# Two directions of a gated linear attention: the second one's gates, scan and keys are issued among the first one's states, in buffers of their own

## The reference, cut to what matters

```python
def gla_chunked(q, k, v, log_a, s0):
    ...
    b = jnp.cumsum(la, axis=3)
    b_last = b[:, :, :, -1:, :]
    q_in = qc * jnp.exp(b)
    k_in = kc * jnp.exp(-b)
    k_end = kc * jnp.exp(b_last - b)
    a_intra = jnp.where(lower, jnp.einsum('bhncd,bhnsd->bhncs', q_in, k_in), 0.0)
    o_intra = jnp.einsum('bhncs,bhnse->bhnce', a_intra, vc)
    chunk_state = jnp.einsum('bhnsd,bhnse->bhnde', k_end, vc)
    chunk_decay = jnp.exp(b_last[:, :, :, 0, :])
    s_final, s_enter = lax.scan(step, s0, (...))
    o_inter = jnp.einsum('bhncd,nbhde->bhnce', q_in, s_enter)
...
    la_cf = gla_log_decay(zac_f, wa2_f, ba_f)      # log_sigmoid(z @ w2 + b2) / 16
    o_f, _ = gla_chunked(Q, K, V, gla_log_decay(za_f, wa2_f, ba_f), s_f)
    o_b, _ = gla_chunked(flip(Q), flip(K), flip(V), flip(gla_log_decay(za_b, wa2_b, ba_b)), s_b)
    y = gla_output(o_f + flip(o_b), g, norm_g)
```

## Time and profile before

| | |
|---|---|
| median of 3 runs | 4089.5 us (4086.95 to 4093.19) |
| profiled execution | 4082.31 us, span 4080.5 us |
| PE busy | 3818.6 us (94%) |
| DVE, ACT, POOL busy | 2399.2, 1682.2, 739.6 us |

### The profile page before, as it was taken

The page is one execution under the profiler, slowest core; times in us unless marked ns, Lnnn a source line. Parts: engine busy times, 40 slices in busy tenths (PEclk is TensorE's granted clock), DMA queues, the critical chain, the costliest instruction groups (busy, mean ns, idle before and its releaser), DMA issues. The chain is left out here.

```text
span 4080.5 us, 57384 instructions
## 1 busy us (share of the span) xinstructions
PE 3818.6 (94%) x23037; PEld 3308.2 (81%) x23037; DVE 2399.2 (59%) x4212; ACT 1682.2 (41%) x2809; POOL 739.6 (18%) x582
## 2 busy tenths in 40 slices
PE   8999989989888879999999999997999999799998
PEld 5788767777787879999999999775777877677887
DVE  6455323447879767777777777556643345674333
ACT  4523332444456883333333333436532233554222
POOL 0112000253104513222233222201000010101000
PEclk9999999989999999999999999998999999899999
DMA  5211334433345459888888887321143432202332
GB/s 206 69 40 43 112 132 176 166 97 92 111 144 166 163 187 307 292 278 285 284 275 287 278 289 226 119 69 52 54 134 114 144 124 89 63 30 83 97 94 78
DMA packets 209193, 617.30 MB, mean 151 GB/s; under 512 B 18464, under 2 KB 68640, under 8 KB 205088
## 3 DMA queue, kind: packets, MB, share of 16 engines
q1 hardware_dynamic: 168352, 465.76, 35.2%
q0 software_dynamic: 40576, 147.87, 10.4%
HBM read 583.67 MB, written 29.88 MB: 150 GB/s over the span
## 5 line engine op out<-in xcount | busy, mean ns | idle before, releaser
L510 DVE TENSOR_TENSOR wlo<-raw,whi 128x1024 fp32r<-128x1024 f32 x576 | 714.7, 1241 | 704.8 <-ACT whi L502 704.2
L544 PE MATMUL ps<-hhi,whi 128*128 128x512 f32 (+1 forms) x2824 | 1075.2, 381 | 12.3 <-ACT uact L3372 8.9
L546 PE MATMUL ps<-hlo,whi 128*128 128x512 f32 (+1 forms) x2824 | 1049.2, 372 | 0.4 <-DVE hlo L2609 0.4
L502 ACT ACTIVATE whi<-raw 128x1024 fp32r<-128x1024 f32 x660 | 693.4, 1054 | 605.4 <-PE ps L555 455.6
L555 PE MATMUL ps<-hhi,wlo 128*128 128x512 f32 (+1 forms) x2824 | 663.2, 373 | 0.0
L544 PEld LDWEIGHTS ps<-hhi,whi 128*128 128x128 f32 x2824 | 533.1, 189 | 115.3 <-issue 22.7
L546 PEld LDWEIGHTS ps<-hlo,whi 128*128 128x128 f32 x2824 | 533.4, 189 | 68.9 <-issue 3.6
L555 PEld LDWEIGHTS ps<-hhi,wlo 128*128 128x128 f32 x2824 | 511.5, 188 | 72.1 <-issue 4.8
L544 PE MATMUL ps<-ag_hi,whi 128*128 128x384 f32 x1024 | 342.1, 334 | 0.0
L546 PE MATMUL ps<-ag_lo,whi 128*128 128x384 f32 x1024 | 342.0, 334 | 0.0
L510 POOL TENSOR_TENSOR wlo<-raw,whi 128x1024 fp32r<-128x1024 f32 x85 | 209.2, 2468 | 328.9 <-ACT whi L502 328.0
(11 more groups left out here) (629 smaller groups left out, 6160.2 us busy)
## 6 DMA issues: line engine op xcount, KB each, us to landing
raw<-w_in SPq DMA_DIRECT2D x151, 512.0 KB, 3.7
raw<-peer_u SPq DMA_DIRECT2D x128, 512.0 KB, 4.6
raw<-peer_v SPq DMA_DIRECT2D x128, 512.0 KB, 4.3
raw<-w_mod SPq DMA_DIRECT2D x96, 512.0 KB, 3.7
raw<-w_gate SPq DMA_DIRECT2D x66, 512.0 KB, 3.6
raw<-w_up SPq DMA_DIRECT2D x66, 512.0 KB, 3.5
raw<-w_down SPq DMA_DIRECT2D x66, 512.0 KB, 3.5
gate_dram<-stage SPq DMA_DIRECT2D x24, 1024.0 KB, 4.7
```

The costliest lines, as they stand in the source:

```text
L502: a.x.activation(whi[n % NW][:], raw[i % NRAW][:], ACT.Copy, bias=0.0, scale=1.0).then_inc(*a.gives("hi", i))
L510: e.x.tensor_tensor(wlo[n % NW][:], raw[i % NRAW][:], whi[n % NW][:].bitcast(F32), ALU.subtract).then_inc(*e.gives(*lo_sig(i)))
L544: t.x.matmul(o, w, p.hi, start=grp.opens and k == 0, stop=False)
L546: t.x.matmul(o, w, p.lo, start=False, stop=False)
```

## The change

The parts of the stream become named steps, and one function, used by all engines, sets their order. Gates and scan of direction 1 (`gates(1)`, `decays(1)`) are laid down around the chunk states of direction 0, its keys (`ends(1)`, `turning(1)`) before direction 0's mix. kin and qin of direction 1 (`keys(1)`) stay behind direction 0's mix, which reads the same two tiles; their multiplication moves into `sums(1)`. Direction 1 has C in the tile gvT (the untransposed values, free once they are turned) and a `dec` of its own. The mark "qk done", which lets `values` 0 begin, moves behind `sums(1)`. No instruction is added or removed in the kernel's code but loads of ACT's function table, which follow from the order: 81 in the program against 79.

```diff
-            self.dec = sb(f"{name}_dec", 8.5 if lat else 8.75, [2, self.NCH])
+            self.dec, self.dec2 = [sb(f"{name}_dec{i}", kb, [2, self.NCH]) for i, kb in
+                                   enumerate((8.5, 8.6875) if lat else (8.75, 8.8125))]
...
+        decs, Cs = [m.dec, m.dec2], [m.C, m.gvT]
+
+        def order(values_by_token, gates, decays, ends, turning, sums, entered, mix, keys):
+
+            yield from values_by_token()
+            yield from gates(0)
+            yield from decays(0)
+            yield from keys(0)
+            yield from ends(0)
+            yield from turning(0)
+            yield from gates(1)
+            yield from sums(0)
+            yield from decays(1)
+            if full:
+                yield from entered(0)
+            yield from ends(1)
+            yield from turning(1)
+            if full:
+                yield from mix(0)
+            yield from keys(1)
+            yield from sums(1)
+            if full:
+                yield from entered(1)
+                yield from mix(1)
...
         def scalar(a):
...
+            def gates(d):
+                C = Cs[d]
                 for i in range(2):
                     a.wait_ge("gla_v", name, "z", d, i)
                 if d:
-                    a.wait_ge("gla_g", name, "kin", 0) if full else a.wait_ge("gla_v", name, "kend", 0)
+                    a.wait_ge("gla_t", name, "gv", 1)
...
-                if d:
-                    a.wait_ge("gla_v", name, "state", 0, NCH - 1, 1)
-                a.x.activation(m.dec[:], C4[:, :, :, 63 if d == 0 else 0], ACT.Exp, bias=0.0, scale=-1.0 / 16).then_inc(
+                a.x.activation(decs[d][:], C4[:, :, :, 63 if d == 0 else 0], ACT.Exp, bias=0.0, scale=-1.0 / 16).then_inc(
...
+            def keys(d):
                 if full:
                     if d:
                         a.wait_ge("gla_t", name, "mix", 0, NT - 2)
-                    a.x.activation(m.kin[:], m.C[:], ACT.Exp, bias=0.0, scale=1.0 / 16).then_inc(*a.gives("gla_a", name, "kin", d))
-                    a.x.activation(m.qin[:], m.C[:], ACT.Exp, bias=0.0, scale=-1.0 / 16).then_inc(*a.gives("gla_a", name, "qin", d))
+                    a.x.activation(m.kin[:], Cs[d][:], ACT.Exp, bias=0.0, scale=1.0 / 16).then_inc(*a.gives("gla_a", name, "kin", d))
+                    a.x.activation(m.qin[:], Cs[d][:], ACT.Exp, bias=0.0, scale=-1.0 / 16).then_inc(*a.gives("gla_a", name, "qin", d))
```

More of the change, by code:

```diff
@@ new lines, in nothing, with steps, values_by_token @@
+        def nothing(count):
+            def steps(*_):
+                for _ in range(count):
+                    yield
+            return steps
+        no_steps = {"values_by_token": nothing(2), "gates": nothing(1), "decays": nothing(1), "keys": nothing(0), "ends": nothing(1),
+                    "turning": nothing(1), "sums": nothing(len(groups)), "entered": nothing((NCH - 1) // 2), "mix": nothing(NT)}
+        def tensor(t):
+            def values_by_token():
+                for i in range(2):
+                    yield When(("evac", place_of["proj", (m, "gv", i)], 0))
+                    yield coming(m.ring, m.there("gv", i))
+                    b = take(t, m.ring, (name, "gv", i), ("gla_v", name, "gv", i))
+                    t.wait_ge(*m.there("gv", i))
+                    for o, s in zip(blocks(b), blocks(m.gvT[:, i])):
+                        ins = t.x.transpose(o, s, ident)
+                    ins.then_inc(*t.gives("gla_t", name, "gv", i))
+                    yield 0.3
+                yield When(("evac", place_of["proj", (m, "za", 0)], 0))
+            def gates(d):
@@ L2002, in tensor, with sums @@
                 yield 0.3
-                if d == 1 and full:
-                    yield Mark((name, "qk done"))
+            def sums(d):
                 for c0, p in groups:
@@ L2017, in tensor, with entered @@
                     yield 0.3
-                if not full:
-                    continue
+                if d == 1 and full:
+                    yield Mark((name, "qk done"))
+            def entered(d):
                 yield Ready(("gla_v", name, "qin", d), ("gla_v", name, "state", d, NCH - 2, 1),
@@ L2060, in tensor @@
                     yield 0.2
+            yield from order(**{**no_steps, "values_by_token": values_by_token, "gates": gates, "decays": decays, "ends": ends,
+                                "turning": turning, "sums": sums, "entered": entered, "mix": mix})
             if not full:
@@ L2075, in scalar, with gates @@
         def scalar(a):
-            for i in range(2):
-                yield
-            for d in range(2):
+            def gates(d):
+                C = Cs[d]
                 for i in range(2):
@@ L2113, in scalar @@
                 yield
-                for _ in groups:
-                    yield
-                if full:
-                    for k in range(NCH - 1):
-                        if k % 2:
-                            yield
-                    for n0 in range(0, NT, 2):
-                        yield
-                        yield
+            yield from order(**{**no_steps, "gates": gates, "decays": decays, "keys": keys, "turning": turning})
             if not full:
@@ L2166, in vector, with ends @@
                 yield
+            def ends(d):
                 v.wait_ge("gla_a", name, "past", d)
@@ L2212, in vector @@
                     yield
+            yield from order(**{**no_steps, "values_by_token": values_by_token, "gates": gates, "decays": decays, "ends": ends,
+                                "sums": sums, "mix": mix})
             if not full:
@@ L2249, in gpsimd @@
                     g.x.tensor_copy(m.r_S[:, d], m.Sen[:, chunks(d)[-1]]).then_inc(*g.gives("gla_g", name, "final", d))
-                if not full:
-                    continue
-                for k in range(NCH - 1):
-                    if k % 2:
-                        yield
-                for n0 in range(0, NT, 2):
-                    yield
-                    yield
+            yield from order(**{**no_steps, "ends": ends, "sums": sums})
             if full:
```

99 lines of the change are left out of this document (49 added, 50 removed).

## The result

The changed kernel takes 4084.1 us (median of 16 runs, 4079.5 to 4089.3), the kernel before 4091.0 in the same sessions (16 runs). The ratio is 0.9983, with a 95% interval of 0.9976 to 0.9990: 6.8 us less (0.17%), between 4 and 10. The forecast was 17 us less. The profiled execution took 4083.1 us, PE busy 3824.9 us, DVE 2405.9, ACT 1684.8, POOL 736.7.

What follows compares the result with a forecast made beforehand. PE is nearly full except in the latent layers' tails, bound by attention-item chains. Per layer 22.5 + 2.5 - 12.4 - 3.1 - 1.1 = 8.4 us, twice 16.8, from 4089.5 to 4072 us; range 4056 to 4087.

Steps and rivals of the forecast that it cites:

- tail shorter: Tail of each latent layer: more item steps done ahead leave 55.4 us of it against 77.9, 22.5 us less.
- operands 2 ready: Tail: the third set of near operands, ready early, no longer delays the copy PE waits 5.3 us for; 2.5 us taken.
- gates and scan in the middle: GLA stream: direction 1's gates ahead of an evacuation and splits on ACT cost PE 0 us, 0 to 2 possible.
- moved matmuls: Projection: scores, transposes, values and rotary matmuls moved in from the tail lengthen it by 12.4 us a layer.
- unit sk, operands 0: Projection: PE waits 3.1 us at sk for a bank ACT evacuates late, and 1.1 for the first near operands.
- rival B: Tail: the shorter tail also stays at 2.4 GHz, up to 8 us more back per layer; about 4056 us, chance 0.14.
- The last mix: Sign of being right: the last GLA mix comes about 14 us before its old place in the units.
- the 12 to 20: Sign of being right: l0's projection longer by 12 to 20 us, with a tail of 52 to 58.
- C, even: Rival: the projection gains what the tail loses, the second near operands exposed whole; 4088.5 us, chance 0.12.
- A: The forecast itself: tails shorten by a third, part paid back in the projection; 4072 us, 4058 to 4083, chance 0.60.
- D's mechanism: Rival, slower: waiting activations hold up slab splits and PE in a circle, from mix 0 to sv; 4102 us, chance 0.09.
- E: Rival: nothing moves, "mixed" comes earlier but the items do not follow; no gain, 4089 us, chance 0.05.

Runs made afterwards that it cites:

- mixed_late_b: Changed kernel with the mark that starts near operands, turned values and first near lane held until three projection units are left in the latent layers; 4095.2 us, ratio 1.0016.
- window_splits_early_b: Changed kernel with copies and low parts of the three window queries issued behind each one's rotary step, not in one tail block; 4073.4 us, ratio 0.9964.
- lane_normed_b: Changed kernel with the first near lane starting on the mark "normed" in place of "mixed"; 4089.3 us, ratio 0.9998.
- ctx_only: Changed kernel with the new order in contexts c0 and c1 alone, the latent layers keeping the old sequence of steps; 4112.8 us, ratio 1.0057.

## Why the forecast missed

The direction was right, and 4084.1 lies in the range (4056 to 4087), but at its upper end: 6.8 us in place of 17, and at 0.17% short of the 0.2% to which the forecast had given 0.74. By its own steps, for a layer:

| term | forecast | measured | from |
|---|---|---|---|
| tail shorter | -22.5 | -22.4 with the next line | 86.2 to 63.8 |
| operands 2 ready | -2.5 | the wait is still 5.1 us | the changed kernel's trace |
| gates and scan in the middle | 0 (0 to 2) | +6.0 | mixed_late_b: 161.9 - 155.9 |
| moved matmuls | +12.4 | +14.9 for these | 176.8 - 161.9 |
| unit sk, operands 0 | +3.1 +1.1 | together | |
| sum | -8.4 | -1.5 | 240.57 - 242.12 |

**The step that failed** is "The gates on ACT in the middle ... 0 taken, 0 to 2 possible. DVE's and PE's parts of these steps are the same instructions in another order." That is where 6.0 of the 6.9 us are that a layer falls short of its forecast. The same instructions in another order put DVE's copy of nk behind 10 us of scans (a wait of 2.1 us), and with the swapped split POOL's product upon DVE's (2.1 us more), each with up to 1.8 us lost at half clock behind it. The forecast had walked down ACT's queue there and not DVE's; a row of that stretch, PE's wait of 0.29 us for the same product in the kernel before, said that this product had no slack at all. And it took no half clock into the projection: rival B counted the clock only as a gain in the tail.

**Operands 2.** The reading of the earlier trace rows was right for the kernel before, and operands 2 are ready early as forecast. But the forecast did not ask what would then stand ahead of the output copy: the block of window splits, which had stood behind it. The wait for `l_o` stayed, 5.1 us for 5.3. A look at what follows that copy on DVE before would have shown a block of 5 us with a PE wait of 4.2 us behind it, and so pointed at what `window_splits_early_b` gained.

**The items' part** came out at 14.9 against 16.6. About 4 of it is a wait with what follows (`lane_normed_b`, whose projection is 4.0 us shorter without it), so by this estimate some 11 us are matmuls, against 12.4. But the wait was neither at sk nor for operands 0. It came 20 us ahead of sk, 2.2 us for a bank behind the normalisation, with a clock of 0.91 behind it. No wait of a unit's matmuls for unit sk is in the table of waits.

**The tail** came out as worked, 55.5 us against 55.4, but in part by luck: the old tail behind that state held PE's wait of 5.3 us for operands 2, and the new one holds a wait of 5.1 us with another cause. Three sets of transposes, two of values and three rotary matmuls were in front of it, and counting how far that state lies into the old tail priced it right. The last mix came 8.6 us before its old place (2749.98 - 2626.05 = 123.9 us after the first L555 group, against 2757.36 - 2624.88 = 132.5) and not 14, since the first two waits lie ahead of it. The projection, 20.9 us longer, lies past the 12 to 20 that the forecast named as its sign.

**The rivals.** C, even, described what happened better than A did: the projection takes back nearly all that the tail gives, 20.9 of 22.4 us; but what it takes beyond the items' matmuls goes by the stream's own waits and the one behind the normalisation, not by operands 1. B fell: the tail's granted clock rose only from 0.76 to 0.82. D's mechanism did not show: no circle of waits, only three single ones. E was out. A's stated span, 4058 to 4083, does not hold its own bounds taken together: at their worst they add 2 x (2.5 + 5.4 + 2) + 3 = 22.8 us to 4072.5, which is 4095.

## To carry to other kernels

When a step is moved in an in-order program, walk down the queue of every engine that it stands on, and look for the neighbour that had no slack before (a wait of 0.3 us is one); here three such neighbours made PE wait 2.1 to 2.2 us each, in all more than a layer gained. Give a wait of the size of these on full PE about twice its length, since matmuls behind it ran at half clock for a while (3.8 us came back for 2.1 removed, 4.0 for 2.2). And where a stage stops in its middle, read what stands on the releasing engine ahead of the releaser: work that only the next stage needs may be moved out; here that gave 7.7 us in the layers, where the change under study gave 3.2. And don't credit the end of such a wait before asking which work steps into its place.

## What had not been expected

- POOL's and DVE's products of two tiles in SBUF, 1.22 and 2.4 us alone, take 3.40 us (DVE) when POOL's began 0.24 us sooner, and 3.23 us (POOL) when it began while a DVE product ran. In these two cases the one that started second paid.
- A wait of 2.1 us in the middle of full-clock work is followed by matmuls 0.43 us apart in place of 0.23, for about 3.6 us. Removing the wait gave 3.8 us.
- An edit that leaves all steps in place but changes what a stream may wait for (`ctx_only`) moved the planner's order enough to cost 12.7 us a layer.
